# x and its remainder start 32 bytes further on in each partition

## The reference

```
h += 0.5 * SwiGLU_1(rms(h))          d_model 1024, hidden 2816
h += Mix_l(rms(h))                   layer 0: gated convolution and mLSTM
                                     layer 1: differential and stick-breaking attention
h += 0.5 * SwiGLU_2(rms(h))
h += sigmoid(rms(h) @ Wg) * (p[l] @ Wp)
```

## Time and profile before

| | |
|---|---|
| median of three runs | 2603.79 us |
| profiled execution | 2601.26 us |
| its span, first to last instruction | 2599.5 us |
| TensorE busy | 2497.4 us, 96% |
| VectorE, ScalarE, GpSimd busy | 32%, 29%, 33% |
| granted TensorE clock, mean | 0.977 |
| DMA | 220.70 MB, 85 GB/s in the mean |

### The profile page before, as it was taken

The page is one execution under the profiler, slowest core; times in us unless marked ns, Lnnn a source line. Parts: engine busy times, 40 slices in busy tenths (PEclk is TensorE's granted clock), DMA queues, the critical chain, the costliest instruction groups (busy, mean ns, idle before and its releaser), DMA issues.

```text
span 2599.5 us, 44514 instructions
## 1 busy us (share of the span) xinstructions
PE 2497.4 (96%) x18512; PEld 2401.3 (92%) x18512; DVE 834.3 (32%) x1318; ACT 759.7 (29%) x904; POOL 856.0 (33%) x260
## 2 busy tenths in 40 slices
PE   7999999979879999999999999999988999999997
PEld 7999999978479999999999999999965799999997
DVE  3220222784652220223422112221176522202224
ACT  4221224123223221223422122331165532212232
POOL 3334334653013333333333333333200133343332
PEclk9999999989779999999999999999989999999999
DMA  4222213411112212212222222233442122222222
GB/s 149 81 82 90 81 68 107 89 56 66 34 62 93 85 65 97 81 63 91 90 81 89 82 89 87 69 112 116 146 122 82 50 91 81 77 93 77 69 81 77
DMA packets 67048, 220.70 MB, mean 85 GB/s; under 512 B 14022, under 2 KB 31302, under 8 KB 51338
## 3 DMA queue, kind: packets, MB, share of 16 engines
q1 hardware_dynamic: 56112, 202.84, 23.5%
q10 hardware_dynamic: 10842, 16.53, 2.2%
HBM read 208.02 MB, written 11.33 MB: 84 GB/s over the span
## 4 chain that ended last, share of the span: by engine, by line
PE 50%; issue 37%; POOL 7%; DVE 3%; ACT 1%; DVEq 0%; POOLq 0%; DMA 0%
PE ps L598 46%; POOL wl L515 7%; PE ps L987 2%; DVE ps L1685 0%; DVE rows L2024 0%; PE ps L873 0%; PE ps L961 0%; PE ps L1017 0%; PE ps L629 0%; PE ps L687 0%; PE ps L865 0%; DVE tiny L2027 0%; PE ps L1007 0%; DVE h L2195 0%; PE ps L645 0%
## 5 line engine op out<-in xcount | busy, mean ns | idle before, releaser
L515 POOL TENSOR_TENSOR wl<-raw,wr 128x2048 fp32r<-128x2048 f32 (+2 forms) x200 | 808.7, 4043 | 1714.3 <-ACT wr L1096 1714.3
L598 PE MATMUL ps<-xr,wr 128*128 128x256 f32 (+1 forms) x2304 | 501.0, 299 | 37.7 <-POOL wl L515 20.1
L598 PE MATMUL ps<-xl,wr 128*128 128x256 f32 (+1 forms) x2304 | 497.2, 298 | 0.0
L598 PE MATMUL ps<-xr,wl 128*128 128x256 f32 (+1 forms) x2304 | 496.8, 298 | 0.0
L1096 ACT ACTIVATE wr<-raw 128x2048 fp32r<-128x2048 f32 (+1 forms) x200 | 351.5, 1757 | 342.0 <-PE ps L598 268.0
L598 PEld LDWEIGHTS ps<-xr,wr 128*128 128x128 f32 x2304 | 391.0, 191 | 40.5 <-issue 36.0
L598 PEld LDWEIGHTS ps<-xl,wr 128*128 128x128 f32 x2304 | 391.6, 191 | 0.0
L598 PEld LDWEIGHTS ps<-xr,wl 128*128 128x128 f32 x2304 | 391.4, 191 | 0.0
L598 PE MATMUL ps<-x2r,wr 128*128 128x256 f32 (+1 forms) x1664 | 354.6, 294 | 1.4 <-POOL wl L515 1.4
L598 PE MATMUL ps<-x2l,wr 128*128 128x256 f32 (+1 forms) x1664 | 353.5, 293 | 0.0
L598 PE MATMUL ps<-x2r,wl 128*128 128x256 f32 (+1 forms) x1664 | 353.5, 293 | 0.0
(11 more groups left out here) (308 smaller groups left out, 1862.0 us busy)
## 6 DMA issues: line engine op xcount, KB each, us to landing
raw<-in_up SPq DMA_DIRECT2D x88, 1024.0 KB, 4.8
raw<-in_down SPq DMA_DIRECT2D x32, 768.0 KB, 4.2
raw<-in_mixin SPq DMA_DIRECT2D x24, 1024.0 KB, 4.8
raw<-in_down SPq DMA_DIRECT2D x32, 640.0 KB, 3.9
raw<-in_ple SPq DMA_DIRECT2D x16, 640.0 KB, 3.8
raw<-in_mixout SPq DMA_DIRECT2D x8, 1024.0 KB, 4.8
kc<-in_kc SPq DMA_DIRECT2D x32, 256.0 KB, 3.5
vc<-in_vc SPq DMA_DIRECT2D x32, 256.0 KB, 2.9
```

The source lines that it names most:

```text
L515: e.tensor_tensor(wl[s][:, 0:p.width], raw[s][:, 0:p.width], wr[s][:, 0:p.width].bitcast(F32), ALU.subtract).then_inc(S(f"w_split{s}"), 1)
L598: mm = e.matmul(piece(u, hf), w_[:, a:b], x_[:, x0:x1], start=n_k == 0 and n_ == 0, stop=n_k == kn_ - 1 and n_ == 2)
```

## The change

Two lines are added. The first moves the place of xr, and with it that of every later tensor, 32 bytes on; the second moves everything behind xl another 32 bytes. So xr and xl (and what is laid on them) start 32 bytes later than before, raw and all that follows 64 bytes later, and h stays. No instruction, wait or transfer is added or taken away.

```diff
     h = sb("h", [P, KD, T])
+    top[0] += 32
     XR_AT = top[0]
     xr = sb("xr", [P, KD, T], F32R)
     xl = sb("xl", [P, KD, T], F32R)
+    top[0] += 32
     RAW_AT = top[0]
     raw = [sb(f"raw{s}", [P, BLK]) for s in range(2)]
```

## The result

The changed kernel is slower: 2609.97 us in the median of 20 runs against 2601.76 us of the kernel before, ratio 1.0029 with a 95% interval of 1.0021 to 1.0037. The forecast was 2593 us, in a range of 2586 to 2607. The changed kernel's profiled execution has a span of 2607.6 us, 8.1 us more than before.

The account below looks back on a forecast made before the run. The prediction took TensorE's matmul pace on line 598 as the bound: 11.5 us saved on xr and xl, less 0.64 hidden in glu, gives 10.8, so 2593.0 us in the median, range 2586 to 2607.

Parts of the forecast that it names:

- 8 cycles a pair, in every pair: Line 598: a pair of matmuls takes 640 cycles on xr, 632 on x2r and hr, throughout the steady stretches.
- The addresses: Streamed tensors sharing the weights' remainder collide with the next weight load and are slow; those 32 bytes off are fast.
- The gate row: 48 gate matmuls stream xr and xl with 36-column weights at 131.7 ns each, taken as evidence for a collision.
- First step: xr and xl 32 bytes off the weights: 6912 matmuls of line 598 save 1.66 ns each, 11.5 us; bounds 0 and 11.5.
- Second step: In the later half of glu, VectorE's convolution hides TensorE's gain: 0.64 us of the saving goes.
- Third step: hr, hl, x2r, x2l, okr and oql, at 96 modulo 128, keep their pace: 0; other bound 16.3 us more.
- Fourth step: ScalarE and VectorE writes of xr and xl, and landings of keys and values, 32 bytes off: taken as 0.
- Slow for where it lies at large: Rival: xr is slow for its region below the weights, so no change, 2601 to 2604 us; no change got 0.15.
- The slower rival: Weights at 64 modulo 128 collide with whatever is streamed; 9792 other matmuls slow too, 16.3 us more, 2620; chance 0.08.
- the trade: Rival: xr gains, the tensors at 96 lose; 5.5 us more, 2609, within 0.3%; chance 0.05.

Follow-up runs that it names:

- first_pad: Kernel before plus only the first added line: everything from xr on 32 bytes later, xr against weights unchanged; timed again, ratio 1.0001.
- second_pad: Kernel before plus only the second added line: xr and xl stay, everything behind xl 32 bytes later; timed again, ratio 1.0031.
- zone_0: Kernel before with only hr, hl, x2r, x2l, okr and oql moved, 224 bytes on, to xr's distance from the weights; 2620.03 us, ratio 1.0076.
- same_timed: Kernel before with 32 bytes added ahead of xr and 96 behind xl, run several times; ratio 0.9971.
- dist64_timed: Kernel before with 64 bytes added ahead of xr and 192 behind xl, run several times; 2591.00 us, ratio 0.9958.
- same_bits: Kernel before with 32 bytes added ahead of xr and 96 behind xl, one execution; 2593.54 us beside 2606.41 for the kernel before.
- dist_64: Kernel before with 64 bytes added ahead of xr and 192 behind xl, one execution; 2593.26 us beside 2598.59.

## Why the prediction was wrong

**What bounds the kernel** was read rightly: the time went with the pace of line 598, and no wait took its place. One reading was too coarse, the "8 cycles a pair, in every pair". In the long stretches on x2r the trace's starts show pairs of about 261 and 266 ns by turns: every second pair is nearly as long as on xr, and most of the gain lies in the others. The timeline hints at it, with spans of 0.43 and 0.42 us by turns on x2r where xr has 0.43:

```profile
900.00 0.42 PE L598 MATMUL ps<-x2r,wl 128*128 128x256 f32 x2
900.26 0.43 PE L598 MATMUL ps<-x2r,wr 128*128 128x256 f32 x2
```

So the match of 8 columns with 32 bytes, which was held against two of the rivals, compared a mean with an address.

**The addresses.** That the place against the weights' group counts was right: first_pad and second_pad tell it from xr's own start, zone_0 from xr and its region. That it is a collision of two reads, as I called it, no run shows. The gate row that spoke for it, 131.7 ns on the same xr, is weaker than it looked: the gates take 131.1 to 131.8 ns in all seventeen profiles, whatever the distances. That fits loads of wr and wl as the other party, but weights of 36 columns may have a pace of their own.

**First step, "modulo 64 a distance of 32 as the fast tensors have".** This failed. The distance went to minus 32, and I took the two for one since 64 divides their difference. The trace of before had only two distances, 0 and 32; a period of 64, 128 or more fitted both. In place of -11.5 us the step cost 1.37 ns x 3456 = +4.7 us by the pairs of the trace, +3.5 to +4.2 by the runs at an equal clock. The bounds, 0 and 11.5 us of saving, should have had a far side above 0: I gave the zone tensors such a bound, not xr.

**Second step.** There was no saving for VectorE to hide; its wait in the kv stage went from 16.2 to 15.9 us. Where xr did become faster, the wait grew as described, to 16.8 us in same_timed and 16.6 in dist64_timed.

**Third step**, the tensors that go to 96 stay as they are, was right. Its other bound, all 9792 matmuls slow for 16.3 us, is close to what zone_0 measured when their distance was made 0: 15.2 us at a clock of 0.976 (2619.8 in three runs, 2604.5 in two of before).

**Fourth step.** Right: ScalarE's operation on xr takes 779 ns as on x2r, keys and values land in 3.3 and 2.8 us.

**The rivals.** 'Slow for where it lies at large' falls with same_bits and dist_64, in which xr runs at 263.3 ns in its old region. The slower rival and the trade both made hr and x2r slower, and these did not change. The case that came, xr slower than before, was in no rival; that the trade's 2609 us is close to the 2609.97 measured is chance, since its loss was to come from the zone. (The range, whose upper end was 2607, left out that 2609 as well, although the trade was counted as within 0.3%.) Of the two rules of the Trainium skill, 16-byte lines (SBUF — State Buffer, Specifications (TRN2)) and independent read ports (TensorE: Matmul & The Clock Gate, Step-by-step: what each phase is for), neither gives a cause for 15 us by a move of 224 bytes, which is a multiple of 16; the measurement decides.

**The clock** was no term of the sum, and some 3.4 of the 8.2 us go with it, by a cause that stays open.

## What to carry to other kernels

Where two equal pieces of code run at steady paces that differ by a few cycles an instruction, compare the places of their operands against each other, not each by itself, and don't extend a rule from two places to a third: here 32 was faster than 0 and minus 32 slower. A row of kernels that move one tensor in steps of 32 bytes shows the whole pattern; here 64 gave 0.9958. And before a difference of 0.3% is explained, put the runs of both kernels against the granted clock.

## What the runs showed of the hardware

The pace of a steady stream of weight loads and matmuls (256 and 320 columns, fp32r) depended on the start of the streamed tensor minus the start of the weights (and of what moved with them): 260.0 to 268.3 ns a pair, 624 to 644 cycles at 2.4 GHz, repeating coarsely after 128 bytes. At one distance a stretch could hold either of two paces (266.7 or 260.0 ns at 128) until its end.
